# Two-layer attention block: the first heads' output squares get a scratch and statistics of their own and come ahead of the panel's squares that fall due at the same place

## The reference, cut to what matters

```python
o = rms_norm(o, out_g) * (1.0 - lam_init)     # o: (1, 8 heads, 256 tokens, 128), attn @ v
y = concatenate([ya * silu(az), yb * silu(bz), yx * silu(xz)])
h = h + y @ w_out
# q and k of each head were normed in the same way, over groups of 64 columns
```

## Time and profile before

| what | value |
|---|---|
| median of 3 runs | 1001.12 us (999.69 to 1004.45) |
| the profiled execution | 1000.91 us, its span 999.1 us |
| TensorE matmul busy | 927.2 us (93%) |
| VectorE busy | 681.2 us (68%) |
| ScalarE busy | 498.6 us (50%) |
| GpSimd busy | 66.8 us (7%) |
| granted TensorE clock, mean | 0.971 of full speed |

### The profile page before, as it was taken

How to read it: one execution, slowest core, us unless ns; L and a number is a source line. 1 busy time by engine, 2 the same in 40 slices (tenths; PEclk the granted TensorE clock), 3 DMA queues, 4 the chain that set the end, 5 groups by cost and what they waited for, 6 DMA issues and landing times.

```text
span 999.1 us, 14688 instructions
## 1 busy us (share of the span) xinstructions
PE 927.2 (93%) x5582; PEld 806.0 (81%) x5582; DVE 681.2 (68%) x1041; ACT 498.6 (50%) x870; POOL 66.8 (7%) x59
## 2 busy tenths in 40 slices
PE   5999898998999799999979898999899599999996
PEld 4798786998888588988869787786687499989885
DVE  5678788778776358788876765758746457764653
ACT  5565555554445355555546545546633644443441
POOL 0201101000000111101111000100001000000000
PEclk9999899999999899999989999999999799999999
DMA  8643643636463646758575656262313256763841
GB/s 310 196 158 122 211 145 112 225 128 226 173 244 117 209 131 208 275 193 268 197 236 185 201 160 189 79 209 86 106 64 117 94 167 213 254 199 96 282 161 43
DMA packets 91815, 174.59 MB, mean 175 GB/s; under 512 B 6733, under 2 KB 11234, under 8 KB 91746
## 3 DMA queue, kind: packets, MB, share of 16 engines
q1 hardware_dynamic: 89248, 166.79, 50.1%
q0 software_dynamic: 1760, 6.24, 1.8%
q10 hardware_dynamic: 738, 0.61, 0.2%
HBM read 172.56 MB, written 1.06 MB: 174 GB/s over the span
## 4 chain that ended last, share of the span: by engine, by line
PE 48%; issue 24%; DVE 17%; ACT 5%; POOL 3%; DMA 2%; SPq 0%; DVEq 0%; POOLq 0%; ACTq 0%
PE acc L1044 9%; PE acc L1046 9%; PE acc L1045 9%; DVE wlo L1679 4%; PE acc L1063 4%; PE acc L1064 4%; PE acc L1065 4%; POOL small L2164 3%; DVE macc L1917 2%; ACT whi L1365 2%; PE tp L1159 1%; DMA raw<-in_o_w_in 1%; DMA raw<-in_e_w_in 1%; DVE small L1724 1%; DVE g L1730 1%
## 5 line engine op out<-in xcount | busy, mean ns | idle before, releaser
L1679 DVE TENSOR_TENSOR wlo<-raw,whi 128x1024 fp32r<-128x1024 f32 (+2 forms) x278 | 324.4, 1177 | 131.0 <-ACT whi L1365 130.3
L1365 ACT CAST whi<-raw 128x1024 fp32r<-128x1024 f32 (+2 forms) x278 | 277.6, 1012 | 148.6 <-PE acc L1046 79.6
L1063 PE MATMUL acc<-xhi,whi 128*128 128x256 f32 x736 | 216.2, 294 | 0.7 <-issue 0.7
L1064 PE MATMUL acc<-xhi,wlo 128*128 128x256 f32 x736 | 210.5, 286 | 0.0
L1065 PE MATMUL acc<-xlo,whi 128*128 128x256 f32 x736 | 210.3, 286 | 0.0
L1044 PE MATMUL acc<-whi,xhi 128*128 128x512 f32 (+1 forms) x352 | 146.1, 415 | 10.4 <-DVE wlo L1679 3.6
L1063 PEld LDWEIGHTS acc<-xhi,whi 128*128 128x128 f32 x736 | 143.5, 195 | 3.5 <-issue 3.2
L1064 PEld LDWEIGHTS acc<-xhi,wlo 128*128 128x128 f32 x736 | 143.5, 195 | 0.8 <-issue 0.5
L1065 PEld LDWEIGHTS acc<-xlo,whi 128*128 128x128 f32 x736 | 143.4, 195 | 0.0
L1046 PE MATMUL acc<-whi,xlo 128*128 128x512 f32 (+1 forms) x352 | 138.3, 393 | 0.0
L1045 PE MATMUL acc<-wlo,xhi 128*128 128x512 f32 (+1 forms) x352 | 137.6, 391 | 0.0
(11 more groups left out here) (332 smaller groups left out, 1205.6 us busy)
## 6 DMA issues: line engine op xcount, KB each, us to landing
raw<-in_e_w_in SPq DMA_DIRECT2D x56, 512.0 KB, 5.7
raw<-in_o_w_in SPq DMA_DIRECT2D x56, 512.0 KB, 5.5
raw<-in_w_mod SPq DMA_DIRECT2D x48, 512.0 KB, 4.3
raw<-in_w_ffn_in SPq DMA_DIRECT2D x40, 512.0 KB, 5.0
raw<-in_w_in SPq DMA_DIRECT2D x28, 512.0 KB, 4.3
raw<-in_w_ffn_out SPq DMA_DIRECT2D x22, 512.0 KB, 4.0
raw<-in_e_w_out SPq DMA_DIRECT2D x16, 512.0 KB, 4.7
raw<-in_o_w_out SPq DMA_DIRECT2D x16, 512.0 KB, 4.3
```

Of the source, the lines that this page charges most:

```text
L1063: mm(o, wh, hi, start=a, stop=False, skip_group_check=True)
L1064: mm(o, wl, hi, start=False, stop=False, skip_group_check=True)
L1365: nc.scalar.copy(whi[:, s.i % SPLIT_SLOTS, 0:s.nk, 0:n], raw[:, s.raw.i % RAW_SLOTS, s.koff:s.koff + s.nk, 0:n]).then_inc(S["hi_ready"], 1)
L1679: tt(wlo[:, slot, 0:s.nk, 0:n], raw[:, s.raw.i % RAW_SLOTS, s.koff:s.koff + s.nk, 0:n], whi[:, slot, 0:s.nk, 0:n].bitcast(F32), ALU.subtra ...
```

## The change

- `panel` takes `heads_first`. If it is set, the steps due at the last sub's position are put down before the panel's evac step gets its place and its semaphore counts. It is set for four panels, those at whose end the `pv` of heads 0, 1, 4 and 5 falls.
- A head's `pv` squares into a tile of its own, `pv_sq` (128x256, a half for each square), with statistics in `pv_stat` (128x3x2). The wait between the two squares goes.
- A head's `pv` no longer takes `scr`. Its squares wait for `on_ready` of the head before (the last reader of `pv_stat`) and for the `pv` matmuls.
- `before_squares` waits for the mean of the last step that used `small`, no longer for that of a head.
- GpSimd's power for a head reads and writes `pv_stat`.

```diff
     def tick(self, st, *names):
...
+        if "ms_ready" in names and st.kind != "pv":
+            st.ms_before, self.stat_ms = self.stat_ms, st.on["ms_ready"]
...
             self.steps.append(Step("sub", sub=sub))
+            if sub.last and pan.heads_first:
+                self.run_due(self.pos)
             if sub.last:
...
                 self.uses(h.f4, "o", "on_ready")
-                self.uses(h.f4, "scr", "sq_ready")
...
-    evs = [pl.panel(W, 512, CW, "x", "norm", gs=64, dst=("g1", 0)),
-           pl.panel(W, 1536, CW, "x", "norm", gs=64, dst=("g1", 1)),
+    evs = [pl.panel(W, 512, CW, "x", "norm", gs=64, dst=("g1", 0), heads_first=True),
+           pl.panel(W, 1536, CW, "x", "norm", gs=64, dst=("g1", 1), heads_first=True),
...
-    evs = [pl.panel(W, 6144, CW, "x", "norm", gs=128, dst=("g0", 0)),
-           pl.panel("e_w_mem_kv", 0, CW, "side", "norm", gs=128, dst=("g0", 1)),
+    evs = [pl.panel(W, 6144, CW, "x", "norm", gs=128, dst=("g0", 0), heads_first=True),
+           pl.panel("e_w_mem_kv", 0, CW, "side", "norm", gs=128, dst=("g0", 1), heads_first=True),
...
+        pv_sq = sb("pv_sq", [P, T], at=nc_at + T * 4)
...
+        pv_stat = sb("pv_stat", [P, 3, NT])
...
             def stat(st, i):
-                return small[:, 3 * (st.on["rstd_ready"] % 3) + i, :]
+                return pv_stat[:, i, :] if st.kind == "pv" else small[:, 3 * (st.on["rstd_ready"] % 3) + i, :]
 
             def before_squares(st):
 
-                wait(("ms_ready", st.on["ms_ready"] - 1))
+                wait(("ms_ready", st.ms_before))
                 wait(st.free["scr"])
...
                 if h.type == "A":
-                    before_squares(st)
+                    wait(("on_ready", st.on["on_ready"] - 1))
                     wait(("o_ps", st.on["o_ps"]))
-                    squares(st, [opsum[:, t * P:(t + 1) * P] for t in range(NT)])
+                    for t in range(NT):
+                        at = slice(t * P, (t + 1) * P)
+                        ins = f(pv_sq[:, at], opsum[:, at], ACT.Square, accum_out=stat(st, 0)[:, t:t + 1])
+                    ins.then_inc(S["sq_ready"], 1)
...
+                ms, to = (pv_stat[:, i, :] for i in (1, 2)) if st.kind == "pv" else (small[:, i + k, 0:n] for k in (1, 2))
                 wait(("ms_ready", st.on["ms_ready"]))
-                nc.gpsimd.tensor_tensor(small[:, i + 2, 0:n], small[:, i + 1, 0:n],
-                                        half_neg[:, 0:n], ALU.pow).then_inc(S["rstd_ready"], 1)
+                nc.gpsimd.tensor_tensor(to, ms, half_neg[:, 0:n], ALU.pow).then_inc(S["rstd_ready"], 1)
```

More of the change, by code:

```diff
@@ L161, in __init__ @@
         self.heads = 0
+        self.stat_ms = 0
         self.gated = {}
@@ L186, in next_acc, with panel @@
         self.acc_uses += 1
-    def panel(self, w, col, ncols, src, evac, orient="tok", kts=KT, opened=False, order=None, put_off=False, **kw):
+    def panel(self, w, col, ncols, src, evac, orient="tok", kts=KT, opened=False, order=None, put_off=False, heads_first=False, **kw):
         pan = Panel(w, col, ncols, src, orient, kts)
+        pan.heads_first = heads_first
         ev = Step("evac_" + evac, panel=pan, **kw)
```

## The result

Changed kernel: 994.51 us, median of 7 runs (990.83 to 997.09). Kernel before, on the same chip: 1003.59 us, median of 7 (999.69 to 1006.62). The ratio is 0.9904, 95% interval 0.9882 to 0.9927, or 9.6 us less (7.3 to 11.8). The forecast was 7.9 us less, 993.2 us. The profiled execution took 995.42 us, its span 993.6 us.

The account below looks back on a forecast made before the run. VectorE with its handoffs was taken as the bound from 83 to 116 and 149 to 190 us; 4.57 + 1.7 + 3.30 - 1.7 = 7.9 us less gave 993.2 us, range 990.2 to 998.5.

Parts of the forecast that it names:

- The bound: From 83 to 116 and from 149 to 190 us, VectorE with its handoffs is the bound, TensorE between them.
- Waits at places 1 and 2: Ends of panels e_w_in:512 and e_w_in:1536: VectorE's three waits go, 2.28 us a place, 4.57 us for two.
- at 3 and 4: Ends of panels e_w_in:6144 and e_w_mem_kv:0: VectorE's two waits go, 1.66 and about 1.65 us, 3.30 us in all.
- The first mod_out: On TensorE, at 115.99 us before: forecast at about 111.4, VectorE deciding, a gain of 4.57 us.
- The fall of the clock behind it: Behind the first mod_out: TensorE's clock no longer falls after the shorter wait, a gain of 1.7 us.
- Transposes of heads 2 and 6: TensorE at places 2 and 4: no more waits for qkT, which were 2.12 and 2.37 us.
- The second mod_out: On TensorE, at 190.31 us before: forecast at about 181, with some 4 us of wait ahead of it.
- The new fall of the clock: Behind the second mod_out, after TensorE's gathered wait: costs 0 to 3.4 us, taken as 1.7 us.
- GpSimd's long power: The panel's power at places 1 and 2, now second: 2.86 us, done at about 87.7, covered by 1.2 us.
- only part arrives: Rival: something held covered is not (panel's power, raw loads or clock falls); gain 2 to 5 us, 996 to 999; chance 0.16.
- The slower rival: Rival: the panel's power holds VectorE's split at places 1 and 2; 1.3 us slower, 1002.4; chance 0.06 with slower otherwise.
- The chain wait: Between a head's two squares on ScalarE: its removal gives 0 to 0.12 us a head, taken as nothing.

Follow-up runs that it names:

- the order alone: Kernel before with the four heads' steps put first, squares still in the shared scratch and statistics: 1000.5 us, ratio 0.9972.
- private tiles alone: Changed kernel without `heads_first` at its four panels, so private scratch and statistics in the old order: 1005.05 us, ratio 1.0017 to the kernel before.
- the second run of the change: The changed kernel unaltered, timed again on the chip of the experiments: 996.32 us, ratio 0.9921 to the kernel before.
- the chain wait kept: Changed kernel with the wait of a head's second square on its first put back: 992.90 us, ratio 0.9910 to the kernel before.
- The shift of mod_out: Changed kernel with the second mod_out due one position later, behind sub 47's matmuls: 988.55 us, ratio 0.9869 to the kernel before.
- last two places: Changed kernel with `heads_first` only at places 3 and 4, the second pair of panels: 1001.04 us, ratio 0.9995 to the kernel before.
- first two places: Changed kernel with `heads_first` only at places 1 and 2, the first pair of panels: 998.03 us, ratio 0.9945 to the kernel before.

## Why the prediction was right, step by step

*The bound.* VectorE with its handoffs bounded the stretch, not TensorE with its 89%: the table follows VectorE's stretches alone, within its intervals. On equal start the second mod_out moves by them too: with the order alone it runs at 187.56 (place 1 starts at 82.39), which is 3.85 us earlier aligned, and the four stretches save 3.9.

*Waits at places 1 and 2: 2.28 us forecast, 2.56 measured; at 3 and 4: 1.65 forecast, 1.84 measured.* The waits were right; the term was sized too small by 0.1 us for each. Back to back, VectorE's rows mostly overlap by 0.07 to 0.1 us (the head's mean ends at 84.86 + 0.16 = 85.02 and the reduce starts at 84.93; the split ends at 86.27 + 1.22 = 87.49 and ytok starts at 87.40), and a wait also loses that overlap. Idle time in brackets does not count it; a stretch from start to start does.

*The first mod_out* was forecast at 111.4, VectorE deciding, with half a microsecond of wait. It runs at 112.59, or 110.9 aligned, with 0.15 us.

*The fall of the clock behind it* was forecast to go. It went: 39.85 us busy of 40 at a clock of 1.00. What it is worth can be read on VectorE, where a split waits for ScalarE's cast and that for TensorE. Before, then after:

```profile
124.59 1.23 DVE L1679 TENSOR_TENSOR wlo<-raw,whi 128x1024 fp32r<-128x1024 f32 x1 [2.33 <-ACT whi L1365]
...
119.70 1.23 DVE L1681 TENSOR_TENSOR wlo<-raw,whi 128x1024 fp32r<-128x1024 f32 x1 [0.97 <-ACT whi L1364]
```

From the reciprocal of place 1 to that of place 3 VectorE took 65.89 us before (81.29 to 147.18) and takes 59.26 after (83.02 to 142.28). That is 6.63 less: 2 x 2.56 for the two stretches and 1.5 for this, where 1.7 was forecast. With private tiles alone the clock did not fall there either (wait of 1.17 us) and the split waits 0.97 us; with the order alone (wait of 1.75 us) it fell, and the split waits 2.33.

*Transposes of heads 2 and 6* no longer wait, as forecast. A transpose not named there waits 1.09 us at 173.77, for ScalarE's g; no fall follows.

*The second mod_out* was forecast at 181, with some 4 us of wait. It runs at 181.59, 179.9 aligned: 8.72 us earlier, 10.45 aligned, where 9.6 were forecast. Of the 10.45 us, 8.8 are the four stretches and 1.5 the fall that went. The slack stands as two waits, 1.09 and 2.92 us, 4.0 in all.

*The new fall of the clock: 1.7 us taken from bounds of 0 and 3.4; 3.4 measured*, in the profile, in the second run of the change and with the chain wait kept. This is the step that was mis-sized, by 1.7 us. It also ate the surplus of the others: aligned, the next wait of TensorE is 234.46 - 228.84 + 1.73 = 7.35 us earlier, and the span's end 5.5 + 1.73 = 7.2 us, near the 7.9 forecast. The shift of mod_out takes wait and fall away together, and in all seven profiles with a wait of 2.90 to 3.04 us there a fall follows.

*GpSimd's long power: 2.86 us under a cover of 1.2 us forecast; 3.81 us and a cover of 0.14 us measured.* VectorE does not wait for it, barely. This is what the rival "only part arrives" spoke of, at its upper edge; the cover held.

*The slower rival* fell by its own mark. At place 1 the split (86.27, 1.22 us) runs beside the power (86.43 to 90.24) and is as long as ever. The same holds with private tiles alone, where the power started 0.10 us after the split. The power, not the split, was stretched, by 0.95 us: at place 1 3.81 against 2.86, at place 3 2.54 against 1.60. The Trainium skill, "SBUF — State Buffer", Who interferes with whom, has each of the two engines lock the other out; as with the rows before, its half on GpSimd agrees and its half on VectorE does not. The order that the rival needs, a power that runs when a split begins, is the one of the earlier trace rows, and there the split took 1.23 us; after, the next split (89.25) begins under the same power, without a wait, and takes 1.22: neither order holds it up.

*The chain wait*: taken as nothing, 0.14 us by the trace, nothing that the runs resolve.

The sum then reads 2 x 2.56 + 2 x 1.84 + 1.7 - 3.4 = 7.1 us, by the trace's alignment 7.2; the two timings of the change gave 9.6 (7.3 to 11.8) and 7.9 (5.4 to 10.3). That 7.9 was forecast is in part luck: the stretches were forecast 0.9 us too small (7.87 against 8.80), and the new fall 1.7 us too cheap. Behind 245 us the two profiled executions differ by single falls of the clock. The lead of the changed kernel, not aligned, shrinks from 5.6 us at 332 to 2.1 us at 646 (645.97 against 648.03 for the same split wait), after falls of 1.7 us each at 560 and 620 that only it has. It is back at 5.5 us at the end, because from 776 to 804 it loses less (granted clock 0.82 against 0.70). Such falls are why the profile alone would not settle the last 2 us.

## What to carry to other kernels

When two pieces of work share a scratch and an order, find the waits of both before removing one: here either half alone gave 2.8 us or nothing, and both gave 8 to 10. Put the short work that is needed soon ahead of the long work that is needed late on every engine that both cross, the small helper engine included. And follow the slack that TensorE gains to the next thing it waits for: gathered into one wait it came with a fall of the clock. Moving the waiting instruction behind a piece of ready work was worth about 5 us more, and as much (6.1 us) in the kernel before, where no fall stood.

## What was not expected of the hardware

Behind the second mod_out a wait of 2.90 to 3.04 us was followed by a loss of 3.4 us at the lower clock in five profiles (the change twice, chain wait kept, last two places, order only), and by 1.7 us in two (first two places, 2.91 us, windows 0.90 and 0.68; private only, 2.90 us, windows 0.75 and 0.83). The loss there came in these two sizes only. After waits of 1.09, 1.17 and 1.49 us nothing was lost.

The length of the wait does not decide it, and neither does the program. The kernel before with mod_out shifted is the kernel before up to the second mod_out. It has the same waits at 105 and 170 us (2.12 and 2.34 us, against 2.12 and 2.37), and no fall behind either, where the earlier trace rows has 0.57 twice. TensorE's busy time, granted clock, DMA share and GB/s in this profile:

```profile
105.00:109.00 4.00, 2.78 (x18) 1.00 0.52 170
169.00:177.00 8.00, 5.61 (x36) 1.00 0.38 122
```

Likewise the last two places alone and the private tiles alone are the same program in the first half. Behind the first mod_out the clock stayed at 1.00 with private tiles (wait of 1.17 us) and fell with the last two places (0.94 us):

```profile
120.00:124.00 4.00, 4.00 (x20) 0.50 0.99 367
124.00:128.00 4.00, 4.00 (x27) 0.69 1.01 368
```

So rows of one trace say what a fall costs, and not whether one comes. The forecast took its odds for the new fall from four rows of a single execution. What decides is not settled by these runs.

GpSimd's power took 0.90 to 1.02 us more when it began while a VectorE split ran (128x2: 0.70 and 1.60 us; 128x8: 1.60 and 2.54; 128x16: 2.86 and 3.81, and 3.88 with private tiles alone), whatever its own length. That is about what was left of the split: at place 1 it ends at 86.27 + 1.22 = 87.49, 1.06 us after the power's start, and the power took 0.95 more; with private tiles alone 1.12 us were left (84.94 + 1.22 against 85.04), and it took 1.02 more. A split that began under a running power lengthened neither, and a power that began under VectorE's reduce (85.10) kept its 0.70 us.
